# Two pieces of TensorE's attention work in another place: the finished head's turn and the next head's first scores

## The reference

```
def attend_block(args):
    qb, blk = args
    ...
    scores = jnp.einsum("bhiqd,bhikd->bhiqk", qb, k).astype(jnp.float32) * scale
    scores = scores - slopes[None, :, None, None, None] * dist
    probs = jax.nn.softmax(jnp.where(allowed, scores, -jnp.inf), axis=-1)
    weights = probs[:, :, 0] - lam * probs[:, :, 1]
    return jnp.einsum("bhqk,bhke->bqhe", weights.astype(v.dtype), v)
...
out = (rms_norm(out, sub_g) * (1.0 - lambda_init)).reshape(b, s, DIFF_WIDTH)
return x + (out * jax.nn.silu(gate)) @ w_out
```

## Time and profile before

| | |
|---|---|
| median of 3 runs | 1218.15 us (1217.96 to 1218.22) |
| the profiled execution | 1218.35 us, its span 1216.7 us |
| PE | 1204.1 us busy, 99% of the span |
| PEld | 1003.6 us, 82% |
| DVE | 910.4 us, 75% |
| ACT | 669.8 us, 55% |
| POOL | 52.1 us, 4% |
| granted TensorE clock | 0.999 of full speed |

### The profile page before, as it was taken

The page is one execution under the profiler, slowest core; times in us unless marked ns, Lnnn a source line. Parts: engine busy times, 40 slices in busy tenths (PEclk is TensorE's granted clock), DMA queues, the critical chain, the costliest instruction groups (busy, mean ns, idle before and its releaser), DMA issues.

```text
span 1216.7 us, 18147 instructions
## 1 busy us (share of the span) xinstructions
PE 1204.1 (99%) x6685; PEld 1003.6 (82%) x6685; DVE 910.4 (75%) x1406; ACT 669.8 (55%) x1098; POOL 52.1 (4%) x46
## 2 busy tenths in 40 slices
PE   8999999999999999999999999999999999999997
PEld 6788888888888887878787789847899888999886
DVE  5888889888965367677777789998798434786776
ACT  6566756675663243655556473675567321577222
POOL 1001210112010000000000000000000000000000
PEclk9999999999999999999999999999999999999999
DMA  6433333423324322222222233123332532332322
GB/s 173 135 95 119 84 107 103 121 70 115 109 70 131 103 87 87 70 70 69 69 75 80 70 87 87 36 70 104 105 104 70 153 89 75 99 107 97 109 88 102
DMA packets 168059, 115.42 MB, mean 95 GB/s; under 512 B 3376, under 2 KB 161360, under 8 KB 166976
## 3 DMA queue, kind: packets, MB, share of 16 engines
q1 hardware_dynamic: 166112, 104.02, 28.8%
q0 software_dynamic: 1888, 10.62, 2.5%
HBM read 112.46 MB, written 2.16 MB: 94 GB/s over the span
## 4 chain that ended last, share of the span: by engine, by line
PE 95%; DVE 3%; DMA 1%; issue 1%; ACT 0%; SPq 0%; ACTq 0%
PE psum L656 54%; PE psum L1189 10%; PE psum L1284 6%; PE psum L926 4%; PE psum L858 4%; PE psum L1032 3%; PE psum L1087 2%; PE psum L895 2%; PE psum L913 1%; PE psum L762 1%; PE psum L770 1%; PE psum L753 1%; PE psum L907 1%; PE psum L744 1%; PE psum L738 1%; PE psum L1101 1%
## 5 line engine op out<-in xcount | busy, mean ns | idle before, releaser
L1320 ACT ACTIVATE w_hi<-w_raw 128x1024 fp32r<-128x1024 f32 x156 | 164.7, 1056 | 275.9 <-PE psum L656 199.6
L1995 DVE TENSOR_TENSOR w_lo<-w_raw,w_hi 128x1024 fp32r<-128x1024 f32 x156 | 190.5, 1221 | 109.2 <-ACT w_hi L1320 108.5
L656 PE MATMUL psum<-a_hi,w_hi 128*128 128x512 f32 (+1 forms) x640 | 227.2, 375 | 0.2
L656 PE MATMUL psum<-a_lo,w_hi 128*128 128x512 f32 (+1 forms) x640 | 222.3, 368 | 0.0
L656 PE MATMUL psum<-a_hi,w_lo 128*128 128x512 f32 (+1 forms) x640 | 221.6, 367 | 0.0
L656 PE MATMUL psum<-b_hi,w_hi 128*128 128x512 f32 x376 | 150.0, 399 | 0.7 <-DVE w_lo L2728 0.4
L656 PE MATMUL psum<-b_lo,w_hi 128*128 128x512 f32 x376 | 148.6, 395 | 0.0
L656 PE MATMUL psum<-b_hi,w_lo 128*128 128x512 f32 x376 | 148.0, 394 | 0.0
L656 PEld LDWEIGHTS psum<-a_hi,w_hi 128*128 128x128 f32 x640 | 115.3, 188 | 24.0 <-issue 3.9
L656 PEld LDWEIGHTS psum<-a_hi,w_lo 128*128 128x128 f32 x640 | 115.0, 188 | 20.7
L656 PEld LDWEIGHTS psum<-a_lo,w_hi 128*128 128x128 f32 x640 | 115.0, 188 | 19.1
(11 more groups left out here) (398 smaller groups left out, 2555.3 us busy)
## 6 DMA issues: line engine op xcount, KB each, us to landing
w_raw<-a_w_in SPq DMA_DIRECT2D x48, 512.0 KB, 3.9
w_raw<-w_down SPq DMA_DIRECT2D x32, 512.0 KB, 3.9
arena<-acs POOLq DMA_DIRECT2D x8, 1024.0 KB, 5.1
w_raw<-a_w_out SPq DMA_DIRECT2D x16, 512.0 KB, 4.1
w_raw<-w_kv SPq DMA_DIRECT2D x16, 512.0 KB, 3.7
w_raw<-b_w_in SPq DMA_DIRECT2D x16, 512.0 KB, 3.9
w_raw<-w_in SPq DMA_DIRECT2D x14, 512.0 KB, 3.9
arena<-w_up SPq DMA_DIRECT2D x7, 1024.0 KB, 5.4
```

The lines of the kernel that those rows point to most:

```text
L656: ins = mm(out, wv[:, u.par, k, :], xv[:, k0 + k, c0:c0 + cn], start=(first and begin and i == 0 and n == 0), stop=(last and end and i == ...
L1320: ac(w_hi[:, u.par, :, :], w_raw[:, u.par, :, :], ACT.Copy).then_inc(S["hi_ready"], 1)
L1995: tt(w_lo[:, u.par, :, :], w_raw[:, u.par, :, :], f32(w_hi[:, u.par, :, :]), ALU.subtract).then_inc(S["lo_ready"], 1)
```

## The change

`turn_out(f)` moves from behind unit 1 to behind unit 2, directly ahead of the ten transposes of `turn_all_weights(s)`. The first scores of head n, which stood at the start of `head(n + 1)` (for the last head after the loop), stand directly behind `all_values(s)` in `head(n)`, in the middle of unit 3. Only head 0's first scores keep their place, inside head 1's unit 0. Both waits of `first_scores` (on `acc_read` and on `wt_ready`) move with it. No other engine's stream is touched.

```
                 if attend and not finish:
                     proj(0, range(2))
-                    first_scores(s, finish)
+                    first_scores(s)
                     proj(0, range(2, KT))
                 else:
-                    if attend:
-                        first_scores(s, finish)
                     proj(0)
...
                 proj(1)
-                if finish:
-                    pe.wait_ge(S["scs_ready"], (s * NT + 3).v)
-                    turn_out(f)
                 if odd_head(n):
                     proj(2)
                 else:
                     pair(2)
                 pe.wait_ge(S["scs_ready"], (s * NT + 3).v)
+                if finish:
+                    turn_out(f)
                 turn_all_weights(s)
...
                 all_values(s, finish)
+                first_scores(n)
                 if odd_head(n):
                     proj(3, range(4, KT))
...
-            def first_scores(s, finish):
-                pe.wait_ge(S["acc_read"], (s * 4 + (M_ATT + (3 if s.reg is not None or s.c > 0 else 4))).v)
-                if finish:
+            def first_scores(s):
+                first = s.reg is None and s.c == 0
+                pe.wait_ge(S["acc_read"], (s * 4 + (M_ATT + (4 if first else 3))).v)
+                if not first:
                     pe.wait_ge(S["wt_ready"], (s * 3).v)
                 scores(s, 0)
                 scores(s, 1)
...
             s, f = Lin(HEADS - 1), Lin(HEADS - 2)
-            first_scores(s, True)
             pe.wait_ge(S["ol_ready"], 4)
```

## The result

The changed kernel takes 1220.99 us (median of 12 runs, 1220.71 to 1223.34) against 1218.23 for the kernel before beside it (12 runs). The ratio is 1.0027, with a 95% interval of 1.0019 to 1.0034: 2.8 us slower.

The account below looks back on a forecast made before the run. TensorE's own steps were taken to bound the kernel. Even heads' stalls of 2.58 us, less 0.36 for odd heads and 0.06 for the turn, gave 2.16 us more, a median of 1220.3 us; range 1219.4 to 1221.4.

Parts of the forecast that it names:

- within 0.2%: Whole kernel: time the same as before to within 2.44 us; chance 0.71.
- the odd heads' gain: First scores behind the value products in heads 1, 3, 5, 7: 0.09 us less each, 0.36 in all, at most 0.72.
- Nothing else is late: Behind the even heads' stall: VectorE and ScalarE each use 0.3 us of slack (1.28 and 1.20), with no further cost.
- The even heads: Heads 2, 4, 6: scores wait for VectorE's value eviction; each loses 0.86 us, 2.58 in all, at most 2.85.
- The turn: Four transposes merged with the ten weight transposes: 0.01 us less in each of six heads, 0.06 in all; later gating free.
- I put 0.09 for the gap before the scores: Odd heads, between value products and first scores: a 0.09 us gap, taken from scores behind projection matmuls.
- the upper: Odd heads' gap before the scores: between 0 and 0.09 us, with 0.09 taken as the top value.
- second place of waiting: Sign of a wrong forecast: TensorE waits somewhere besides the scores' wait for VectorE's value eviction; no size given.
- The stall is longer than its parts: Even heads, VectorE's eviction end to first score product: over 0.09 us beyond the assumed 0.06; 1221.0 or 1221.4; chance 0.26.
- Nothing ran ahead of the waiting scores: Even heads, rival: 24 projection matmuls start while scores wait, so the stall vanishes; 0.7 us less, 1217.5; chance 0.06.

Follow-up runs that it names:

- second median: The changed kernel, unaltered, run once more beside the kernel before; 1221.47 us, ratio 1.0025.
- the own wait: Changed kernel, but loop heads' first scores wait only for two tiles read and the gated turn, not three tiles; 1218.74 us, ratio 1.0005 against the kernel before.
- one tile between: Changed kernel, but even heads' first scores stand one value-projection tile (12 matmuls) later, same wait; 1218.60 us, ratio 1.0006 against the kernel before.

## Why the prediction was right or wrong

The prediction gave 2.16 us more and put most of the chance on "within 0.2%"; measured were 2.8 (2.99 by H and P), over 2.44. It was wrong on that side. The first median, 1220.99, lies in its range of 1219.4 to 1221.4, but by luck as to the cause: the range was stretched for a longer stall that did not come. The second median, 1221.47, lies just above it. The two steps that failed are the odd heads' gain (0.36 us forecast, 0.03 measured) and "Nothing else is late" (nothing forecast, 0.44 measured). By its steps:

- *The even heads* were right in mechanism and size. Forecast 0.86 each, 2.58 in all; with their scores alone moved it was 0.88 each, 2.64 in all. TensorE started 0.06 us behind VectorE, as taken. The experiments with the own wait and with one tile between show both that this wait is the cause and that it could have been covered.
- *The turn* was right: 0.06 us less, VectorE's later gating free.
- *The odd heads* failed in the step "I put 0.09 for the gap before the scores". The gap behind value products is 0.17, and the four heads give 0.03 in place of 0.36. The prediction called 0.09 "the upper", taking the price behind a matmul of another shape as a ceiling; it was none. Changing the tiling mode drains the engine, by "TensorEngine Tiling (Array Packing)" of the Trainium skill, section Key Properties. Read as the prediction read it, that nothing is gained while the number of switches stays the same, it came out: the trace agrees in the sum, 0.01 us per odd head. No run changes the number of switches, so that a drain is the cause of the 0.09 and the 0.17 is not shown.
- *"Nothing else is late"* is the step that failed most: 0.44 us, a term put at nothing. The prediction followed VectorE's evictions after unit 3, and not ScalarE's high half of the next weights, which waits for the end of that unit too. In the loop this cost VectorE 0.76 of its 1.28 us of slack instead of the 0.3 forecast, without harm. For head 7 the same chain runs into the output projection, which the prediction did not look at: there a wait of TensorE for VectorE already stood in the earlier trace rows, which says that no slack was left. VectorE's weight half behind head 7 was 0.73 us late; at the last scores' bias 0.45 of that was left, counted from head 7's value products, and it reached TensorE in two places: 0.16 at an add that it had not waited for before, 0.27 at the wait that it had. The first of these is the second place of waiting that the prediction named as a sign of being wrong.
- *The rivals.* "The stall is longer than its parts" named times near the one that came, 1221.0 and 1221.4, but not by its mechanism: the hand-over was 0.06. Nothing ran ahead of the waiting scores, and the stall did not vanish.

What stays open: the medians of the two sets of runs of the changed kernel stand 2.8 and 3.3 over theirs of before, H and P give 2.99, and H, P and M together 2.81. M varies between profiles, from 206.48 to 207.01, at the wait for a transfer that is named above; the last tenths of the medians are not assigned.

## What to carry to other kernels

Before moving work ahead of a unit, ask for each of its waits who counts it last: a count of "tiles read" made the scores wait for a tile that they don't use, and a wait that was free behind 24 matmuls cost 0.85 us directly behind the work that releases it. Follow every engine that waits for the end of the unit that is pushed back, here ScalarE's weight halves, and follow it past the loop: a slack that absorbs the delay in each turn may be missing after the last one. A wait that the bound engine already has shows a place without slack: here 0.27 of the 0.44 us came out there, the rest shortly before.

## What the runs showed that was not expected

- The toll at TensorE's change from 128 to 64 rows depends on what stands ahead: 0.09 us behind the projections' matmuls, 0.17 behind the value products (2.32 to the scores against 2.15 to a projection), 2.32 or 2.33 in all nine kernels that have scores there without a wait. What causes it is not shown.
- The idle time in a timeline's bracket is less than what a wait costs from start to start: 0.30 shown for 0.55, 0.78 shown for 0.86, and nothing shown for 0.16, since a matmul's row ends behind the start of the next regular one (rows of 0.40 us at steps of 0.23 in the earlier trace rows).
